# Dense kind's tiles ahead of the scan's features, masks of two heads in one operation, and the levels' query products on GpSimd

## The reference

```python
(a_q, a_i, a_ff, a_fb, b_q, b_k, b_v, c_q, c_k, c_v, d_q, d_k, d_v, g_lat) = jnp.split(h @ w_in, SPLIT_AT, axis=-1)
y_a, yc_a = hgrn2_mixer(a_q, a_i, a_ff, a_fb, ..., lb, hg_norm_g, ctx_out)      # scan, two directions
qB = apply_rope(rms_norm(split_heads(b_q, GA_HEADS), ga_qn), rope64)            # dense kind "b"
kB = apply_rope(rms_norm(split_heads(b_k, GA_KV), ga_kn), rope64)
...
qC, kC, vC = diff_qk(c_q, n, True), diff_qk(c_k, n, True), split_heads(c_v, DF_HEADS)   # kind "c": rope only

def step(s, xs):                                # gla_chunk_scan, per head, f = gate, k = 1 - f
    bcum = jnp.cumsum(fc, axis=1)               # fc = log f
    o_inter = jnp.einsum('bthk,bhkv->bthv', qf * jnp.exp(bcum), s)
    att = jnp.einsum('bthk,bshk,btshk->bhts', qf, kf, decay)   # decay = exp(bcum_t - bcum_s), s <= t
    ...
```

## Time and profile before

| | us |
|---|---|
| median of 3 runs | 2372.48 (2372.2 to 2372.6) |
| the profiled execution | 2378.82 |
| its span, first to last instruction | 2377.0 |
| PE busy | 2030.4 |
| DVE busy | 1231.1 |
| ACT busy | 782.0 |
| POOL busy | 57.5 |

### The profile page before, as it was taken

How to read it: one execution, slowest core, us unless ns; L and a number is a source line. 1 busy time by engine, 2 the same in 40 slices (tenths; PEclk the granted TensorE clock), 3 DMA queues, 4 the chain that set the end, 5 groups by cost and what they waited for, 6 DMA issues and landing times.

```text
span 2377.0 us, 27355 instructions
## 1 busy us (share of the span) xinstructions
PE 2030.4 (85%) x10304; PEld 1436.9 (60%) x10304; DVE 1231.1 (52%) x2754; ACT 782.0 (33%) x1668; POOL 57.5 (2%) x98
## 2 busy tenths in 40 slices
PE   4777987999789586887998859977989997999999
PEld 1766864545444275775555424545578885887887
DVE  2386275645555748355655454883644443433333
ACT  3322333544431242333554211112543323323222
POOL 1100000000000100000000200000000000000000
PEclk8889998999899888898999978997899998999999
DMA  7201201010461311111010431112023332333331
GB/s 266 33 18 36 63 19 36 1 36 10 135 246 54 68 36 36 45 36 36 1 36 1 131 85 51 55 45 54 1 85 95 95 99 61 89 98 98 96 95 66
DMA packets 149025, 157.33 MB, mean 66 GB/s; under 512 B 5596, under 2 KB 110208, under 8 KB 148896
## 3 DMA queue, kind: packets, MB, share of 16 engines
q1 hardware_dynamic: 142464, 135.81, 18.8%
q0 software_dynamic: 6432, 19.78, 3.0%
HBM read 151.37 MB, written 4.19 MB: 65 GB/s over the span
## 4 chain that ended last, share of the span: by engine, by line
PE 67%; DVE 20%; ACT 6%; issue 3%; DMA 2%; POOL 1%; DVEq 0%; ACTq 0%; SPq 0%; POOLq 0%
PE psum L1172 10%; PE psum L1173 10%; PE psum L1174 10%; PE psum L744 6%; PE psum L773 5%; PE psum L939 5%; PE psum L1070 4%; PE psum L972 3%; PE psum L953 3%; PE psum L707 2%; DVE stats L1967 2%; PE psum L760 2%; PE psum L761 2%; PE psum L762 2%; ACT arena L1458 1%
## 5 line engine op out<-in xcount | busy, mean ns | idle before, releaser
L1172 PE MATMUL psum<-part,part 128*128 128x512 f32 (+1 forms) x1072 | 417.0, 389 | 51.2 <-DVEq L1739 23.2
L1173 PE MATMUL psum<-part,part 128*128 128x512 f32 (+1 forms) x1072 | 414.9, 387 | 0.0
L1174 PE MATMUL psum<-part,part 128*128 128x512 f32 (+1 forms) x1072 | 414.1, 386 | 0.0
L1269 ACT ACTIVATE arena<-psum 128x384 f32<-128x384 f32 (+7 forms) x435 | 170.9, 406 | 570.1 <-PE psum L707 228.9
L2302 DVE TENSOR_TENSOR part<-arena,part 128x1024 fp32r<-128x1024 f32 x112 | 137.3, 1226 | 251.5 <-ACT part L1269 251.5
L1172 PEld LDWEIGHTS psum<-part,part 128*128 128x128 f32 x1072 | 205.5, 192 | 94.4 <-issue 30.3
L1269 ACT ACTIVATE part<-arena 128x1024 fp32r<-128x1024 f32 (+1 forms) x212 | 193.2, 939 | 205.7 <-PE psum L1174 140.9
L744 PE MATMUL psum<-arena 128*128 128x512 f32 (+2 forms) x576 | 227.0, 553 | 8.9 <-ACT arena L1269 4.6
L1174 PEld LDWEIGHTS psum<-part,part 128*128 128x128 f32 x1072 | 205.4, 192 | 40.7
L1173 PEld LDWEIGHTS psum<-part,part 128*128 128x128 f32 x1072 | 205.8, 192 | 39.7
L1967 DVE TENSOR_REDUCE stats<-psum 128x1 f32<-128x768 f32 (+6 forms) x208 | 138.8, 709 | 157.5 <-PE psum L939 156.1
(11 more groups left out here) (272 smaller groups left out, 2460.9 us busy)
## 6 DMA issues: line engine op xcount, KB each, us to landing
arena<-in_w_in SPq DMA_DIRECT2D x80, 512.0 KB, 4.1
arena<-in_w_mlp SPq DMA_DIRECT2D x64, 512.0 KB, 3.8
arena<-in_w_ada SPq DMA_DIRECT2D x48, 512.0 KB, 5.7
arena<-in_w_gate SPq DMA_DIRECT2D x32, 512.0 KB, 4.0
arena<-in_w_out SPq DMA_DIRECT2D x24, 512.0 KB, 3.7
arena<-in_w_branch SPq DMA_DIRECT2D x8, 512.0 KB, 3.7
arena<-in_x POOLq DMA_DIRECT2D x4, 512.0 KB, 9.2
arena<-in_x POOLq DMA_DIRECT2D x1, 2048.0 KB, 8.7
```

The costliest lines, as they stand in the source:

```text
L1172: pe.matmul(dst, lo, x_hi_, start=first, stop=False)
L1173: pe.matmul(dst, hi, x_lo_, start=False, stop=False)
L1174: return pe.matmul(dst, hi, x_hi_, start=False, stop=last)
L1269: return act.activation(dst, src, ACT.Copy)
```

## The change

Three edits, all in the scan stages.

1. In t = 0 the dense kind's blocks come first in the weight ring, its six tiles are made before `scan_inputs` on PE, ACT and DVE (`AHEAD`), and POOL copies their context queries before it clears the scan's arrays. The stream has 12 tiles left, two before the scan and ten beside it, paced 10 over 12 steps (`PACE`); t = 1 keeps 11 over 9. Splits and places follow the new order.
2. DVE's masked copy takes both heads of a group at once, from two adjacent banks.
3. The product of the exponentials with the queries (nine per scan, at 768 columns, or 512 in layer 1 and at level 8) is made by POOL. PE waits for it beside DVE's keys before each level's product, and before the outputs.

The hunks left out repeat `layer` and `scan_inputs` as shown for ACT and DVE.

```diff
@@ -182,11 +182,12 @@
     for l in range(DEPTH):
         w = a["w_in"][l]
         for t in range(2):
+            if t == 0:
+                rows(("b", l), w, C_B, 512)
             for name, c in (("q", C_AQ), ("f", C_FF), ("b", C_FB)):
                 cols(("hg", l, t, name), w, c + P * t)
             if t == 0:
                 rows(("ai", l), w, C_AI, 256, 4)
-                rows(("b", l), w, C_B, 512)
                 rows(("c", l), w, C_C, 512)
             else:
                 rows(("cv", l), w, C_CV, 256, 4)
@@ -489,18 +490,23 @@
             return terms
 
         def stream_tiles(t):
-            return [(tag, m) for tag in (("ai", "b", "c") if t == 0 else ("cv", "d")) for m in range(TT)]
+            return [(tag, m) for tag in (("b", "ai", "c") if t == 0 else ("cv", "d")) for m in range(TT)]
 
         def input_blocks(l, t):
 
-            names = (("ai", 2), ("b", 4), ("c", 4)) if t == 0 else (("cv", 2), ("d", 4))
-            return [("hg", l, t, name) for name in "qfb"] + [(name, l, i) for name, n in names for i in range(n)]
-
-
-        HI_PLACES = (("free", "o", "v0", "v1", "q0", "q1", "free", "o", "v0", "v1", "q0", "q1", "v0"),
+            features = [("hg", l, t, name) for name in "qfb"]
+            if t == 0:
+                return [("b", l, i) for i in range(4)] + features + [("ai", l, i) for i in range(2)] + [("c", l, i) for i in range(4)]
+            return features + [("cv", l, i) for i in range(2)] + [("d", l, i) for i in range(4)]
+
+
+        HI_PLACES = (("free", "o", "v0", "v1", "q0", "q1", "free", "o", "v0", "v1", "q0", "q1", "free"),
                      ("free", "q0", "q1", "s0", "s1", "s2", "free", "s0", "s1"))
-        SPLIT_BEFORE = ({1: (6,), 2: (7,), 3: (8,), 6: (9, 10), 12: (11, 12)}, {1: (5,), 2: (6,), 6: (7, 8)})
-        SPLIT_WITH = (5, 4)
+        SPLIT_BEFORE = ({0: (1, 2, 3), 1: (4,), 2: (5,), 7: (9,), 8: (10,), 9: (11,), 10: (12,)}, {1: (5,), 2: (6,), 6: (7, 8)})
+        SPLIT_WITH = ({1: (6,), 2: (7,), 3: (8,)}, {0: (1,), 1: (2,), 2: (3,), 3: (4,)})
+
+        AHEAD = (TT, 0)
+        PACE = ((12, 2 * TT - 2), (9, 2 * TT - 1))
 
         def block_before(l, t, j):
 
@@ -837,7 +843,8 @@
                 for level in range(FIRST_STATE):
                     E = e_s[level % 2]
                     pe.wait_ge(*scan_dve.at("e", l, t, level))
-                    level_mm(level, E[:, 1], E[:, 0], lambda g: scan_dve.at("level", l, t, level, g))
+                    pe.wait_ge(*scan_pool.at("queries", l, t, level))
+                    level_mm(level, E[:, 1], E[:, 0], lambda g: scan_dve.at("level", l, t, level, g - g % 2, g - g % 2 + 1))
                     yield True
                 pe.wait_ge(*scan_dve.at("e", l, t, FIRST_STATE))
                 for g in range(scan_groups(l) // 2):
@@ -857,8 +864,9 @@
                 yield True
                 make_states(("context",), [[(ROWS_AT["context"] + CT * d + c, LT + c) for c in range(CT)] for d in range(2)])
                 yield True
-                pe.wait_ge(*scan_dve.at("level", l, t, FIRST_STATE - 1, scan_groups(l) - 1))
+                pe.wait_ge(*scan_dve.at("level", l, t, FIRST_STATE - 1, scan_groups(l) - 2, scan_groups(l) - 1))
                 pe.wait_ge(*scan_act.at("state", l, t, "context"))
+                pe.wait_ge(*scan_pool.at("queries", l, t, N_LEVELS - 1))
                 for j in range(last_q_of(l)):
                     b = banks["o", j]
                     open_bank(b)
@@ -1042,11 +1050,13 @@
 
             def layer(l):
                 for t in range(2):
+                    beside = stream(l, t)
+                    for _ in range(AHEAD[t]):
+                        next(beside)
                     scan_inputs(l, t)
-                    beside = stream(l, t)
                     next(beside)
                     next(beside)
-                    alongside(scan(l, t), 14 if t == 0 else 9, beside, 18 if t == 0 else 11)
+                    alongside(scan(l, t), PACE[t][0], beside, PACE[t][1])
...
@@ -1309,8 +1319,8 @@
 
             def scan_inputs(l, t):
                 for n, (name, s, t0, t1) in enumerate(hg_tiles(l)):
-                    if n < SPLIT_WITH[t]:
-                        split_input(l, t, n + 1)
+                    for j in SPLIT_WITH[t].get(n, ()):
+                        split_input(l, t, j)
                     act.wait_ge(*mm_done.at("hg", l, t, name, s))
                     dst = q_s[:, t0:t1] if name == "q" else f_s[:, 0 if name == "f" else 1, t0:t1]
                     act.activation(dst, bank(s)[:, 0:t1 - t0], ACT.Sigmoid).then_inc(scan_act((name, l, t, s)), 1)
@@ -1381,7 +1391,7 @@
                 read_states(("context",), 2, STATE_AT["context"])
                 yield True
                 if t == 0:
-                    act.wait_ge(*mm_done.at("weights", ring.number("b", l, 2)))
+                    act.wait_ge(*mm_done.at("weights", ring.number("ai", l, 0)))
                 for j in range(last_q_of(l)):
                     act.wait_ge(*scan_mm.at("o", l, t, j))
                     copy(o_a[:, j, t * P:(t + 1) * P], bank(banks["o", j])[:, 0:P]).then_inc(scan_act(("o", l, t, j)), 1)
...
@@ -1821,14 +1833,13 @@
                     sf, sb = halves(f_s[:, 0, 0:n], h), halves(f_s[:, 1, 0:n], h)
                     rf, rb = halves(r_s[:, 0, 0:n], h), halves(r_s[:, 1, 0:n], h)
                     ek = halves(E[:, 1, 0:n], h)
-                    w, m = n // (2 * h), min(n, nq)
+                    w = n // (2 * h)
                     dve.wait_ge(*scan_act.at("e", l, t, level))
                     dve.tensor_tensor(rf[:, :, 0], rf[:, :, 0], sf[:, :, 1, h - 1:h].to_broadcast([P, w, h]), ALU.add).then_inc(scan_dve(), 1)
                     dve.tensor_tensor(rb[:, :, 1], rb[:, :, 1], sb[:, :, 0, 0:1].to_broadcast([P, w, h]), ALU.add).then_inc(scan_dve(), 1)
                     dve.wait_ge(*scan_dve.now())
                     dve.tensor_tensor(sf[:, :, 1], sf[:, :, 1], sf[:, :, 0, h - 1:h].to_broadcast([P, w, h]), ALU.add).then_inc(scan_dve(), 1)
                     dve.tensor_tensor(sb[:, :, 0], sb[:, :, 0], sb[:, :, 1, 0:1].to_broadcast([P, w, h]), ALU.add).then_inc(scan_dve(("update", l, t, level)), 1)
-                    dve.tensor_tensor(E[:, 0, 0:m], E[:, 0, 0:m], q_s[:, 0:m], ALU.mult).then_inc(scan_dve(), 1)
                     dve.tensor_tensor(ek[:, :, 0], ek[:, :, 0], halves(kf_s[:, 0:n], h)[:, :, 0], ALU.mult).then_inc(scan_dve(), 1)
                     dve.tensor_tensor(ek[:, :, 1], ek[:, :, 1], halves(kb_s[:, 0:n], h)[:, :, 1], ALU.mult).then_inc(scan_dve(("e", l, t, level)), 1)
 
@@ -1840,16 +1851,17 @@
                 for level in range(N_LEVELS):
                     if level < N_LEVELS - 1:
                         decays(level + 1)
-                    for g in range(scan_groups(l) if level < FIRST_STATE else 0):
+                    for g in range(0, scan_groups(l) if level < FIRST_STATE else 0, 2):
                         lo_tile, hi_tile = group_tiles(g)
-                        n = hi_tile - lo_tile
-                        dve.wait_ge(*scan_mm.at("level", l, t, level, g))
+                        n, b = hi_tile - lo_tile, banks["level", level, g]
+                        dve.wait_ge(*scan_mm.at("level", l, t, level, g + 1))
                         if level == 0:
-                            dve.wait_ge(*scan_act.at("base", l, t, g))
+                            dve.wait_ge(*scan_act.at("base", l, t, g + 1))
                         else:
-                            dve.wait_ge(*scan_dve.at("level", l, t, level - 1, g))
-                        dve.copy_predicated(att[:, g % 2, lo_tile:hi_tile, :], bc(level_mask[:, level, :], 1, [P, n, P]),
-                                            bank(banks["level", level, g])[:, 0:n * P].rearrange("p (j n) -> p j n", n=P)).then_inc(scan_dve(("level", l, t, level, g)), 1)
+                            dve.wait_ge(*scan_dve.at("level", l, t, level - 1, g, g + 1))
+                        mask = level_mask[:, level, :].unsqueeze(1).unsqueeze(1).to_broadcast([P, 2, n, P])
+                        dve.copy_predicated(att[:, :, lo_tile:hi_tile, :], mask,
+                                            psum[:, b:b + 2, 0:n * P].rearrange("p h (j n) -> p h j n", n=P)).then_inc(scan_dve(("level", l, t, level, g, g + 1)), 1)
...
@@ -2431,6 +2445,16 @@
+            def copy_queries(l, tiles):
+
+                for tag, m in tiles:
+                    if tag in HEADS and LT <= m < last_q_of(l):
+                        nq = HEADS[tag][0] * HEADS[tag][2]
+                        q_dst = {"b": q_b, "c": q_c, "d": q_d}[tag][:, m, :]
+                        pool.wait_ge(*rows_act.at("raw", tag, l, m))
+                        pool.wait_ge(*keys_ready(tag, l, m))
+                        pool.tensor_copy(placed(tag, q_dst), in_groups(raw[raw_turn(l, tag, m) % 2][:, 0:nq])).then_inc(rows_pool(("q", tag, l, m)), 1)
+
@@ -2439,16 +2463,18 @@
...
                 for t in range(2):
```

(16 more changed lines are left out.)

16 lines of the change are left out of this document (10 added, 6 removed).

## The result

The changed kernel takes 2375.47 us (median of 20 runs, 2370.95 to 2381.56); the kernel before, run beside it on the same chip, 2370.19 us (20 runs). The ratio is 1.0022, 95% interval 1.0015 to 1.0029: slower by 4 to 7 us. Forecast were 24 us less.

A forecast was written before the change was run, and what follows sets the result against it. No engine is full: scans are lock steps of three engines, DVE setting the pace in the first for some five steps. Terms -16.3, -13.0, +3 and +2 give -24.3 us: 2372.5 to 2348 us, range 2338 to 2358.

The forecast's parts named there:

- term 2: New t = 0 scan with ten tiles beside it: 92 us in layer 0, 79 in layer 1, between two prices.
- the price by DVE's chain: t = 0 scans priced by DVE's operations, with stretches before and behind: 8.1, 55.1, 24.5, sum 87.7 us; layer 1 73.6.
- The price by likeness: t = 0 scans priced from the similar t = 1 scan (100.4 us in layer 0): 96 us, and 84 in layer 1.
- The middle between the two prices: t = 0 scans taken at 92 us, between 87.7 and 96, and in layer 1 at 79, between 73.6 and 84.
- the sum of -24.3: Whole kernel: -16.3 and -13.0 us in the t = 0 stages, +3 and +2 in the t = 1 stages.
- Products on POOL: Scan levels: POOL and DVE take turns; each product costs DVE 1.5 us, saves 0.87; at 512 columns 1.05 against 0.60.
- terms 3 and 4: t = 0 stages: tiles ahead of the features 32.6 and 27.4 us; start and related waits 8.3 and 12.2.
- The rival in which the tiles don't run beside the head rows: Tiles ahead: coupled row buffers make a tile take 8.7 us, not 6.5; ten lose 22 us: 2370 us, 12%.
- +3 and +2: t = 1 stages of layers 0 and 1: +4 and +3 us from POOL's products, less 1 each for joined masks.
- Masks: Scan levels: joining two heads' copies saves 0.15 us a level, 1 us a scan.
- The slower one: Every scan level: POOL's product, at 3.0 us (2.0 at 512 columns), is the bound; 44 us more, 2392 us, 12%.
- the deduction of 7: Layer 0, t = 0 scan priced from t = 1: 7 us off 100.4, since 10 tiles over 12 steps leave fewer bare levels.

The follow-up runs named there:

- k1: Query products left out on every engine, against the kernel with only the dense tiles ahead (2356 us): 2345.40 us, ratio 0.9887 to the kernel before.
- k2: Six c tiles per layer with 8 matmuls in place of 24, against the kernel with only the dense tiles ahead (2356 us): 2342.47 us.
- e1: The whole change with the query products back on DVE, against the kernel before: 2360.30 us, ratio 0.9954.
- f3: t = 0 tiles paced 11 over 9 steps in place of 10 over 12, against the kernel with only the dense tiles ahead (2356 us): 2356.59 us.
- e4: The kernel before with only the dense tiles ahead, masks and products as before: 2356.26 us, ratio 0.9948.
- e2: The kernel before with only the query products moved to POOL: 2389.02 us, ratio 1.0083.
- k3: The whole change (2375 us) with the splits of the dense blocks 1 to 3 ahead of the gains wait: 2356.69 us, ratio 0.9938.
- f4: Seven spare POOL products per layer that nobody needs, DVE keeping its own, against the kernel with only the dense tiles ahead: 2369.53 us, ratio 0.9998.

## Why the prediction was wrong

1. **The new scan (term 2), the step that failed.** 92 and 79 us were forecast, 102.4 and 87.5 measured. What was wrong is the price by DVE's chain (87.7 and 73.6), which took DVE as the engine that sets every step and let PE's tiles lie beside it. The kernel after in the three parts of that price, layer 0:

```profile
147.70:156.10 8.40, 7.54 (x72) 7.25 (x72) 1.25 (x2) 6.17 (x12) 0.00 (x0) 1.00 0.00 0
156.10:217.00 60.90, 46.10 (x314) 38.66 (x314) 54.41 (x77) 16.96 (x37) 15.72 (x8) 0.86 0.06 18
217.00:250.10 33.10, 27.41 (x160) 24.18 (x160) 9.20 (x17) 11.46 (x32) 2.32 (x3) 0.90 0.21 64
```

   8.1, 55.1 and 24.5 us were forecast. DVE's work in the levels was priced right: it is busy 54.4 us there. Missing are 6.0 us in which it waits for ACT's read of a tile (ACT itself waits there for PE's tiles), and 8.6 us behind the levels, where DVE is busy for 9 us of 33: PE is busy for 27 and waits for 6, and 24.5 with no wait were priced. Layer 1 has the same: 7.8, 55.3 and 24.4 us, forecast 8.1, 48.0 and 17.5. k1 and k2 agree: DVE's and PE's work are both on the path. That DVE set the pace with the dense heads in the scan was read from the earlier trace rows and not tested. The price by likeness (96 and 84) was nearer. It had 3 and 2 us for POOL where taking the products back brings 6.0 and 4.4 in these scans, and it took 7 us off the half t = 1, of which e1 (96.4 and 83.1 against 100.4 and 89.0) shows 4 and 6; f3 shows that the spread of the tiles is not the reason. The middle between the two prices then carried half of the chain's error.

   Of the sum of -24.3, about +14 stood for POOL (7 in the t = 0 scans, 7 in t = 1) and -4 for the masks, so about -34 for the order alone; e4 measured -12 (-16 to -9).
2. **Products on POOL.** The mechanism was right, and the sum nearly: about +14 forecast, +15 on top of the rest and +20 alone measured. In 61 to 1120 us the first two of the four lines of updates, after and with the products back on DVE:

```profile
L1839 DVE TENSOR_TENSOR arena<-arena 128x384 f32<-128x384 f32 x32 | 42.1, 1315 | 0.0
...
L1838 DVE TENSOR_TENSOR arena<-arena 128x384 f32<-128x384 f32 x32 | 26.4, 826 | 32.5 <-ACT arena L1348 32.1
```
```profile
L1836 DVE TENSOR_TENSOR arena<-arena 128x384 f32<-128x384 f32 x32 | 17.7, 554 | 35.9 <-ACT arena L1346 35.4
L1837 DVE TENSOR_TENSOR arena<-arena 128x384 f32<-128x384 f32 x32 | 17.6, 551 | 0.0
...
L1841 DVE TENSOR_TENSOR arena<-arena 128x768 f32<-128x768 f32 x16 | 15.2, 950 | 0.0
L1841 DVE TENSOR_TENSOR arena<-arena 128x512 f32<-128x512 f32 x20 | 13.7, 683 | 0.0
```

   68.5 us against 35.3: 33.2 us of blocking in the updates alone, for 28.9 us of products saved. In all DVE is busy 19.2 us more (1247.3 against 1228.1), so the blocking is 44 to 48 us (the products' share of the busy time is 25.2 by k1, 28.9 as a sum of durations), 1.2 to 1.3 a product. Forecast was a block of 1.5 us against a saving of 0.87, and 1.05 against 0.60 at 512 columns. So the net cost per product was near the forecast. Not forecast was where it falls. The block stands mostly on the updates, for which the next exponentials wait, while the saved product stands behind them. And in t = 1 nearly all of the cost falls in layer 0: the scan of t = 1 takes 106 us in layer 0 in all three kernels with products on POOL (this one, e2, k3) and 100 in the ten others that have them on DVE; in layer 1 the same scan is only about 1 us longer. Forecast were +4 and +3 less the masks.

   POOL's product was forecast at 1.5 and 1.05 us. Where nothing held it up it took 1.80 to 1.85 us at 768 columns and about 1.27 at 512; its groups have means of 2.04 and 1.47, because it mostly waits for DVE's running operation first. Both forecasts were about a fifth too low. f4's spare product took 1.47 us; it reads one tile twice and writes another, and which of these makes it shorter no run shows.
3. **Tiles ahead and the start (terms 3 and 4), right.** From PE's first matmul behind the barrier (63.1 and 820.7 us; before 63.1 and 819.3) to the first level product (147.8 and 904.0; before 105.4 and 863.0) it is 42.4 and 39.6 us longer; forecast were 40.9 and 39.6. The rival in which the tiles don't run beside the head rows is out. What I did not draw from it is that most of the 12 us of idle could be had by moving the splits ahead of the wait for the gains.
4. **t = 1.** +3 and +2 forecast; +7.9 in layer 0 and -0.7 in layer 1 by the stages of single runs, +6.0 and +0.2 by the scan parts. The sum is near, the division between the layers was wrong.
5. **Masks.** 2 us were counted for t = 0, and 1 in each t = 1 stage; nothing that can be told from zero.
6. **The rivals.** The slower one had POOL's product as the bound of every level, from 2.35 us on. It named the side on which the time came out, but not the reason: the products stayed below that (2.23 at most), and PE never waited for them. The instruction ahead of the first product took 14 ns and lay 9 us before it. What was missing is a rival in which PE's tiles set part of the scan; the likeness without the deduction of 7 (103 and about 91) would have given some 23 us more, 2371, though with too much for the order and too little for POOL. The prediction's own signs had it too: both scans of t = 0 were to be over 50 us shorter, and they were 47 and 44.

Open is how much of the 15 to 20 us is the longer chain of updates and how much the blocked head rows; f4 has both.

## What to carry to other kernels

Before you price work that leaves an engine at its duration, leave it out and time that: it is the most the move can bring, here 11 to 21 us for 29 us of products. GpSimd is no free second VectorE: an SBUF product there stopped SBUF products on VectorE until it was done, so in a kernel like this one it belongs beside operations that read PSUM, or into a gap, and never at the head of the chain on which the next step waits. And when a reorder shows a new idle stretch, look at what stands queued behind the wait; here two moved loops were worth 17 to 20 us, and the whole reorder had brought 12 to 14. And when one engine's work is taken out of a lock step, price the rest by each of the engines that are left, the stretch behind the last level included.

## What the runs showed of the hardware

- The change's GpSimd product took 1.80 to 1.85 us at 768 columns and about 1.27 at 512 where nothing held it up; one with the same tile as both inputs took 1.47 at 768.
- Beside masked copies from PSUM on VectorE neither was slowed (1.47 and 1.99 us, 1.81 and 1.91 us). Beside SBUF products whichever came second waited: up to 2.3 us on GpSimd, and up to 2.2 us for a 0.42 or 0.55 us operation on VectorE.
- A level's masked copies cost the same joined or not: 1.91 us for two, of 1024 and 512 columns, and 1.98 for four, two of 512 and two of 256.
- With less TensorE work in a stretch its granted clock there was lower, 0.81 against 0.93, and a 512-wide matmul took 496 ns in place of 400 to 418.
